# Mixer: 16 transfers for a tile of x, 8 for its latents, contiguous block transposes, and new orders of work

## The chip, the cores and the metric

One core of a Trainium2 chip runs the whole kernel in one launch. The metric is the device time of a launch in microseconds (us). All data are float32. The engines are named by what they do: TensorE multiplies matrices, VectorE and ScalarE work element by element, GpSimd helps, and the queue SP issues DMAs.

## The reference, cut to what matters

One layer of a streaming encoder over a prompt of 2048 frames and a sample of 32. The change touches its first stage only, the mixers:

```python
proj = jnp.einsum('bsd,de->bse', x, w_in)            # one projection of x for both mixers
c_q, c_kv, k_pe, pr = proj[..., :384], proj[..., 384:640], proj[..., 640:672], proj[..., 672:]
q = jnp.einsum('bsl,lhe->bshe', rms_norm(c_q, q_norm_g), w_uq)
ckv = rms_norm(c_kv, kv_norm_g)                      # the latents, also an output
kpe = apply_rope(k_pe, cos, sin)                     # also an output
attn = mla_prompt(q_nope, q_pe, ckv, kpe, w_ukv, pos)
rw, wkv_fin = rwkv7_mixer(pr, wkv0, shift0, ...)     # a recurrence, done in blocks of 64 rows
out = jnp.einsum('bsm,md->bsd', concatenate([attn, rw]), w_o)
```

Behind it come a layer norm, a top-2-of-32 mixture of experts and another layer norm.

## The kernel before

The kernel runs stage after stage: the mixer (here), attention, the router, the experts, the last norm. The mixer goes over 17 tiles of 128 rows (16 of the prompt, one with the sample). Its constants and the whole of `w_in` stay in SBUF.

Each tile passes three stages, written as Python generators: `project` (letter a) multiplies `xT`, the tile of x transposed, with `w_in`, normalises queries and latents and stores them; `rwkv` (b) does the recurrence; `heads_out` (c) normalises its heads. `layered()` joins them on every engine: a turn of the loop runs stage a of tile i, b of tile i - 1 and c of tile i - 2. Turns 0 and 1 and the two last ones (17 and 18, the drain, which have no stage a) are written out, the 15 between are a loop. Within a turn each engine's order is a string: each letter takes that stage's generator to its next `yield`. These are PE_ORDER, ACT_ORDER, VEC_ORDER and SP_ORDER, at lines 59 to 63. Engines wait for each other by named steps (`t.w(vec, "v_turned")` waits for a step of the same tile, `t.w0` for that of the tile before, `t.arrived` for a group of DMAs).

The steps that the text speaks of, by line:

- SP: first x at 519, then the weights and constants up to 536 (`w_g` at 532), the x load of later tiles in `x_load` (539 to 543), token moves of v, b and k between partitions (551), `first` and `rope` (566, 567), the stores of kpe and ckv (570, 571), of the latents to their output (`ckv_out`, 576), kpe_out (577), edge, qn and qp (581 to 591), `masks`, `keep` and `s_init` (602 to 604), and the state's store (622). In a turn SP issues the three inputs of b first, then `first` and `rope`, the tokens, kpe and ckv, the latents' stores, qn, qp, then x for the tile after next, and the state.
- VectorE: squares summed for the norms (`sq_sum`, 1067 to 1070), `pr_edge` (1075, waits for `first` and `rope`), `ckv_turned` (1097), `q_roped` (1104), `xT` (1109); the mixing of rows (1118: u_low, u_k, u_r, u_v), `u_pad` (1128, waits for masks, keep and s_init), `g_sig` (1131), `v_turned` (1136), ..., `kk_norm2` (1157), `kk_rs` (1160), `a_hat`, `b_hat`, `b_turned` (1174), `k_hat` (1177), then the levels of the block inverse (Z and U); of the heads y_centred (1245), `y_rs` (1248), `y_normed` (1250) and the gating (1253 to 1255).
- ScalarE: `cq_sq`, `ckv_sq`, kp4 (689 to 693), the copies pr3, pr1, pr0, pr2 (702), tanh, exponentials, `kk_root` (764).
- TensorE: the projection, 19 column blocks of 8 matrix products, each block in two halves (806), kpe_sum (847, waits for kp4), rms_sums (851, waits for sq_sum), q_nope and q_pe (872, 880); lora_w and lora_a (960), lora_g (967, waits for g_sig), kk_norm and bonus_sum (894), and the recurrence (901 to 1018). The group of columns k=0 needs the bank of k=3, so it waits for the copy pr3.

Every 32 columns of a VectorE transpose are turned within their 32x32 blocks. x is therefore loaded such that the blocks fall in place: rows j*4+g of the tile in partitions 32q + j.

Of the kernel before, what the change touches and what calls it, by code (L numbers as in the profile page):

```python
# [30 lines left out]
P = 128  # L31
# [8 lines left out]
CQ, CKV = QL // P, KVL // P  # L40
# [3 lines left out]
KC = D // P  # L44
# [11 lines left out]
LEVELS = 6  # L56


PE_ORDER = ("aacaabcaaaaaaabaaabaaaaaaaaaaaaaaabababbbaabaaababbbabababab"
            "abababaababbbabbbb")  # L60
ACT_ORDER = "bbbcbbcbbbaabbbbbaacaaaabbbabbb"
VEC_ORDER = "bcbbbbbcbabbbbbcabbbbbcbbbbbbbbbbbabbabababbbbbabaab"
SP_ORDER = "bbcaabbbacaaaaab"


# [318 lines left out]
def mixer(nc, io, scr):  # L384
    ahead = scr["first_of_attention"] = first_of_attention(nc)

    with ExitStack() as ctx:
        def sb(name, shape, dt=F32):
            return ctx.enter_context(nc.sbuf_tensor("mx_" + name, shape, dt))
# [24 lines left out]
        x = sb("x", [P, D])  # L414
# [7 lines left out]
        xT = sb("xT", [P, KC, P])  # L422
# [4 lines left out]
        ckv = sb("ckv", [P, CKV, P])  # L427
# [7 lines left out]
        cw, kw = sb("cw", [P, 4 * CKV, 32]), sb("kw", [32, P])  # L435
# [45 lines left out]
        first_x, first_xT = (ctx.enter_context(nc.semaphore("mx_first_" + n)) for n in ("x", "xT"))  # L481
        biases = ctx.enter_context(nc.semaphore("mx_biases"))
        selected = ctx.enter_context(nc.semaphore("mx_selected"))
        x_in = Dmas(nc, ctx, "mx_x_in", 4)
        a_in = Dmas(nc, ctx, "mx_a_in", 2)
        b_in = Dmas(nc, ctx, "mx_b_in", 3)
        mla_out = Dmas(nc, ctx, "mx_mla_out", 13, 1)
        v_in, bt_in, kt_in = (Dmas(nc, ctx, f"mx_{n}_tokens", 8, 1) for n in "vbk")
        rwkv_out = Dmas(nc, ctx, "mx_rwkv_out", 1, 1)
        edge_out = Dmas(nc, ctx, "mx_edge_out", 1, 1)  # L490
# [5 lines left out]
        def row(ap, i):  # L496
            return ap[bass.ds(i, 1)].rearrange("a p n -> p (a n)")
# [17 lines left out]
        @block.sync  # L515
        def _(sp):
            sp.dma_start(ident[:], io["ident"]).then_inc(ident_in, 16)
            for q in range(4):
                x_in.go(sp.dma_start(x[32 * q:32 * q + 32], io["x"][0, 32 * q:32 * q + 32]))
            for c0, c1 in ((0, QL + KVL), (PE_COL, PE_COL + ROPE)):  # L520
                sp.dma_start(w_in[:, :, c0:c1], w_src[:, :, c0:c1]).then_inc(w_part[4], 16)
            early.go(sp.dma_start(par[:], io["par"]))
# [15 lines left out]

            def x_load(tile):

                for q in range(4):
                    x_in.go(sp.dma_start(x[32 * q:32 * q + 32].rearrange("j (n i) -> j n i", i=32),
                                         tile.rearrange("(j g) (k a i) -> j (g k) a i", g=4, a=4, i=32)[:, :, q, :]))

            def tokens(d, dst, src):

# [10 lines left out]
            def project(t):  # L557
                t.ahead((avec, "xT", 0), (avec, "q_rope_sin", -1), (avec, "kpe_roped", 0), (avec, "ckv_turned", 0),
                        (aact, "q_nope", 0), (avec, "q_roped", 0), (aact, "edges", 0))
                i = t.i if isinstance(t.i, int) else sp.snap(t.i)  # L560
                after = i + 2 if isinstance(i, int) else sp.snap(t.i + 2)
                col = bass.ds(i * P if isinstance(i, int) else sp.snap(t.i * P), P)
                yield

                t.w0(avec, "q_rope_sin")
                a_in.go(sp.dma_start(first[:], row(io["first"], i)))
                a_in.go(sp.dma_start(rope[:], row(io["rope"], i).rearrange("p (a n) -> p a n", a=2)))
                yield
                t.w(avec, "kpe_roped")
                mla_out.go(sp.dma_start(scr["kpeT"][:, col], kpe[:]))  # L570
                mla_out.go(sp.dma_start(scr["ckvT"].rearrange("(c p) n -> p c n", p=P)[:, :, col], ckv[:]))
                t.w(avec, "ckv_turned")
                yield
                tile = io["ckv_out"][bass.ds(i, 1)].rearrange("a (i b) (c r j) -> (a i) (b c) r j", b=4, c=CKV, r=4)
                for q in range(4):
                    mla_out.go(sp.dma_start(tile[:, :, q, :], cw[32 * q:32 * q + 32]))
                mla_out.go(sp.dma_start(io["kpe_out"][bass.ds(i, 1)].rearrange("a (b i) j -> i (a b) j", b=4),
                                        kw[:].rearrange("i (b j) -> i b j", b=4)))
                yield
                t.w(aact, "edges")  # L580
                edge_out.go(sp.dma_start(row(io["edge_out"], i), edge[:].rearrange("p a n -> p (a n)")))
                yield
                t.w(aact, "q_nope")
                qd = scr["qT"]
                for h2 in range(2):
                    mla_out.go(sp.dma_start(qd.rearrange("(c b) d n -> b d c n", b=2)[h2, 0:NOPE, :, col],
                                            qn[h2 * 64:h2 * 64 + 64]))
                yield
                t.w(avec, "q_roped")
                for h4 in range(4):  # L590
                    mla_out.go(sp.dma_start(qd.rearrange("(c b) d n -> b d c n", b=4)[h4, NOPE:QK, :, col],
                                            qp[h4 * 32:h4 * 32 + 32]))
                yield
                t.w(avec, "xT")
                x_load(io["x"][bass.ds(after, 1)].rearrange("a p n -> (a p) n"))

            def rwkv(t):
# [73 lines left out]
        def _(a):  # L671
# [124 lines left out]

            layered(a, NT, (("a", 0, aact, project), ("b", 1, act, rwkv), ("c", 2, oact, heads_out)), ACT_ORDER)

        @block.tensor
        def _(pe):  # L800
# [84 lines left out]

            heads = [(q, r, slice(64 * r, 64 * r + 64)) for q in range(4) for r in range(2)]
            blocks = [(4 * c + q, q, slice(64 * c, 64 * c + 64), hs) for c in range(2) for q, _, hs in heads]

            def by_halves(dst, w, src):
# [163 lines left out]
            pe.wait_ge(w_part[4], 32)  # L1053
            layered(pe, NT, (("a", 0, aten, project), ("b", 1, ten, rwkv), ("c", 2, oten, heads_out)), PE_ORDER)

        @block.vector
        def _(v):
# [5 lines left out]
            def project(t):  # L1063
# [18 lines left out]
                for c in range(CQ):  # L1082
                    ins = v.scalar_tensor_tensor(out=cq[:, c, :], in0=b4[2][:, c, :], scalar=qg[:, c:c + 1],
                                                 in1=msr[:, 0, :], op0=ALU.mult, op1=ALU.mult)
# [3 lines left out]
                for c in range(CKV):  # L1088
                    ins = v.scalar_tensor_tensor(out=ckv[:, c, :], in0=b4[3][:, c, :], scalar=kvg[:, c:c + 1],
                                                 in1=msr[:, 1, :], op0=ALU.mult, op1=ALU.mult)  # L1090
# [3 lines left out]
                do(v.tensor_tensor(kpe[:], b4[2][32:64, 3, :], rope[32:64, 1, :], ALU.mult), "kpe_sin")  # L1094
                do(v.tensor_tensor(kpe[:], kpe[:], kpe2[0:32, :], ALU.add), "kpe_roped")
                yield
                v.transpose(cw[:].rearrange("p (b c) j -> p b c j", b=4), ckv[:].rearrange("p c (i b) -> p b c i", b=4))
                t.mark(v.transpose(kw[:], kpe[:]), "ckv_turned")
                yield

# [5 lines left out]
                t._wait(x_in, None, 1)  # L1106
                t.w(aten, "pr_proj2")
                for g in range(4):
                    ins = v.transpose(xT[:, :, g:P:4], x[:, 256 * g:256 * g + 256].rearrange("p (k i) -> p k i", k=KC))
                t.mark(ins, "xT")  # L1110

            def rwkv(t):
# [129 lines left out]
            def heads_out(t):  # L1242
# [12 lines left out]
                do(v.tensor_tensor(ys[:], ys[:], gk[:], ALU.mult), "gated")  # L1255

            layered(v, NT, (("a", 0, avec, project), ("b", 1, vec, rwkv), ("c", 2, ovec, heads_out)), VEC_ORDER)


# [1370 lines left out]
```

## Time and profile before

| | us |
|---|---|
| median of 3 runs | 3352.1 |
| lowest and highest | 3346.84, 3356.85 |
| profiled execution | 3348.55 |
| its span | 3346.5 |

The page gives, for one profiled execution, the busy time of each engine (PE is TensorE, DVE is VectorE, ACT is ScalarE, POOL is GpSimd, SPq is the queue SP that issues DMAs, PEld the weight loads) and 40 slices of the span of 83.7 us with the busy share in tenths. The mixer is slices 1 to 17 and a part of 18. The mean granted clock of TensorE over the span is 0.947.

### The profile page before, as it was taken

What the parts mean: (1) busy time and instruction counts of PE and PEld (TensorE: products, weight loads), DVE (VectorE), ACT (ScalarE), POOL (GpSimd) and SP (SyncE); (2) the same over time, 40 slices, a digit from 0 to 9 for tenths busy, and PEclk for the clock granted to TensorE, in tenths of its full rate; (3) what the DMA queues carried; (4) which work ended last, traced back from release to release, by engine and by line L of the source; (5) the groups of instructions that cost most, each with busy time, mean ns of one, the idle gap of its engine ahead of it and who ended that gap; (6) DMA issues with size and microseconds to landing.
All of it is one profiled execution on the core that took longest, in us unless ns stands there. A gap on an engine that the chain in (4) does not pass through costs nothing. (4 is left out here: it accounts for less than half of the span.)

```text
span 3346.5 us, 74487 instructions
## 1 busy us (share of the span) xinstructions
PE 2949.8 (88%) x26600; PEld 2235.1 (67%) x26601; DVE 1750.7 (52%) x3820; ACT 971.1 (29%) x2500; POOL 581.9 (17%) x875
## 2 busy tenths in 40 slices
PE   7999999999999999669898898989975999999991
PEld 6888888888888888545555555545544776666770
DVE  1666666666666666648686886822234222222225
ACT  2333333333333333224343434412210111111115
POOL 0000000000000000000000000001113555545650
PEclk9999999999999999779999999999987999999995
DMA  6111111111211111420101000033325898886447
GB/s 188 34 37 36 36 36 36 36 37 37 38 37 37 36 36 36 96 84 1 38 1 35 5 21 15 1 108 128 125 85 219 272 342 289 246 257 171 100 93 244
DMA packets 337220, 310.25 MB, mean 93 GB/s; under 512 B 235200, under 2 KB 290528, under 8 KB 322528
## 3 DMA queue, kind: packets, MB, share of 16 engines
q1 hardware_dynamic: 315424, 238.88, 23.4%
q0 software_dynamic: 21504, 67.13, 8.9%
q8 instruction: 226, 3.70, 0.5%
q14 instruction: 66, 0.54, 0.1%
HBM read 208.12 MB, written 84.42 MB: 87 GB/s over the span
## 5 line engine op out<-in xcount | busy, mean ns | idle before, releaser
L806 PE MATMUL mx_bank<-mx_xT,mx_w_in 128*128 128x128 f32 x5168 | 661.2, 286 | 71.1 <-issue 52.4
L806 PEld LDWEIGHTS mx_bank<-mx_xT,mx_w_in 128*128 128x128 f32 x5168 | 618.8, 198 | 144.1 <-issue 121.0
L1497 PE MATMUL at_bank<-pl_kT,pl_qT 128*128 128x512 f32 (+5 forms) x656 | 293.8, 534 | 2.4 <-DVE at_vals L1621 2.4
L1469 ACT ACTIVATE at_PQ<-at_bank,at_nms 128x512 f32<-128x512 f32 (+5 forms) x328 | 192.8, 596 | 277.6 <-DVE at_nms L1597 199.9
L2288 PE MATMUL ex_down<-ex_wd,ex_hT 128*128 x512 | 235.6, 603 | 28.1 <-ACT ex_hT L2217 26.4
L2165 POOL DMA_INDIRECT ex_x<-scr_hx,ex_idx x256 | 247.0, 965 | 68.3 <-issue 59.4
L2264 PE MATMUL ex_gate<-ex_wg,ex_xT 128*128 x1024 | 233.2, 381 | 19.0 <-SPq L2137 18.8
L2264 PEld LDWEIGHTS ex_gate<-ex_wg,ex_xT 128*128 128x128 f32 x1024 | 195.4, 191 | 72.9 <-issue 49.0
L2224 ACT ACTIVATE ex_y<-ex_down,ex_gcol 128x512 f32<-128x512 f32 x128 | 81.0, 683 | 543.8 <-POOL ex_gcol L2172 227.2
L2264 PE MATMUL ex_up<-ex_wu,ex_xT 128*128 x1024 | 231.6, 379 | 0.0
L1640 DVE COPY at_PT<-at_bank 128x512 f32<-128x512 f32 (+3 forms) x328 | 196.8, 601 | 55.0 <-PE at_bank L1509 41.0
L1528 PEld LDWEIGHTS at_bank<-at_PT,at_vals 128*64 128x64 f32 (+1 forms) x2208 | 118.4, 138 | 155.2 <-issue 80.9
L2333 DVE STREAM_TRANSPOSE ex_xT<-ex_x 128x256 f32<-128x256 f32 x256 | 141.1, 609 | 147.2 <-DMA ex_x<-scr_hx,ex_idx 147.2
L1509 PE MATMUL at_bank<-pl_at_ident,at_PQ 128*128 128x128 f32 x1104 | 187.4, 285 | 32.4 <-ACT at_PQ L1469 15.9
L1509 PEld LDWEIGHTS at_bank<-pl_at_ident,at_PQ 128*128 128x128 f32 x1104 | 126.8, 142 | 120.3 <-issue 57.2
L2264 PEld LDWEIGHTS ex_up<-ex_wu,ex_xT 128*128 128x128 f32 x1024 | 190.3, 191 | 23.2
L657 POOL TENSOR_TENSOR mx_AR<-mx_u,mx_ep 128x512 f32<-128x512 f32 x17 | 20.0, 1176 | 1036.2 <-DVE mx_kh L1154 1036.2
L1593 DVE TENSOR_REDUCE at_mx<-at_bank 128x1 f32<-128x512 f32 (+5 forms) x328 | 188.4, 574 | 11.8 <-PE at_bank L1497 7.3
L1528 PE MATMUL at_bank<-at_PT,at_vals 128*64 128x128 f32 (+1 forms) x2208 | 168.0, 285 | 26.0 <-DVE at_o_sb L1615 25.8
L2288 PEld LDWEIGHTS ex_down<-ex_wd,ex_hT 128*128 128x128 f32 x512 | 96.6, 192 | 132.9 <-issue 130.8
L702 ACT ACTIVATE mx_pr<-mx_bank 128x256 f32<-128x256 f32 (+1 forms) x68 | 37.0, 544 | 510.1 <-PE mx_bank L806 500.8
L2340 DVE SCALAR_TENSOR_TENSOR ex_th<-ex_th,ex_gate 128x256 f32<-128x256 f32 x64 | 26.8, 419 | 261.3 <-ACT ex_th L2212 201.0
(316 smaller groups left out, 4738.6 us busy)
## 6 DMA issues: line engine op xcount, KB each, us to landing
ex_wg<-in_w_eg SPq DMA_DIRECT2D x32, 1024.0 KB
ex_wu<-in_w_eu SPq DMA_DIRECT2D x32, 1024.0 KB
ex_wd<-in_w_ed SPq DMA_DIRECT2D x32, 1024.0 KB
mx_x<-in_x SPq DMA_DIRECT2D x76, 128.0 KB, 4.0
pl_ro_x<-in_x SPq DMA_DIRECT2D x17, 512.0 KB, 3.9
scr_hx<-ro_h SPq DMA_DIRECT2D x17, 512.0 KB, 2.7
scr_acc<-ro_ha SPq DMA_DIRECT2D x17, 512.0 KB, 2.9
co_r<-scr_acc SPq DMA_DIRECT2D x17, 512.0 KB, 5.6
```

The lines of the kernel that those rows point to most:

```text
L806: ins = pe.matmul(dst, w_in[:, k, col:col + n], xT[:, k, :], start=(k == 0), stop=(k == KC - 1))
L1469: ins = a.activation(PQ[:, n % NP, 0:full], b[:, 0:full], ACT.Exp, bias=bias, scale=SCALE, accum_out=sums[:, j, h, 1 + gi:2 + gi])
L1497: t.mark(pe.matmul(bank[n % SB][:, 0:wd], qT[h][keys(h), j * P:(j + 1) * P], kT[h][keys(h), k0 * P:k0 * P + wd], start=True, stop=True), f ...
L1509: ins = pe.transpose(bank[SB + n % TB][0:rows, c:c + P], PQ[:, n % NP, c:c + rows], ident[:, :])
L1528: ins = pe.matmul(bank[7][64 * h:64 * h + 64, 0:P], vals[0:rows, k0 + s, 64 * h:64 * h + 64], PT[0:rows, m % NPT, s, :], start=(gi == 0 an ...
L1593: t.do(v.tensor_reduce(mx[:, 1 + gi:2 + gi], b[:, 0:wd], AX.X, ALU.max), f"max{n}")
L1640: ins = v.tensor_copy(PT[:, n % NPT, 0:full, :], b[:, 0:full * P].rearrange("p (a n) -> p a n", a=full))
L2165: x_in[s].go(g.indirect_dma_start(x[s][:, k, :], None, rows, bass.IndirectOffsetOnAxis(ap=idx[s][:, k:k + 1], axis=0)))
L2224: ins = a.activation(y[s][:, 512 * n:512 * n + 512], down_b[n][:, :], ACT.Copy, scale=gcol[s][:, 0:1])
L2264: ins = pe.matmul(b[s][:, 0:FE], xT[s][:, k, :], wv[:, k * FE:(k + 1) * FE], start=(k == 0), stop=(k == KC - 1))
L2288: ins = pe.matmul(down_b[n][:, :], hT[s][:, m, :], wv[:, m * D + n * 512:m * D + (n + 1) * 512], start=(m == 0), stop=(m == FC - 1))
L2333: ins = v.transpose(xT[s][:, :, 32 * h:32 * h + 32], x[s][:, h, :].rearrange("p (i k) -> p k i", k=KC))
```

## The change

- x: each tile's load is cut by row groups as well. Where four transfers took every fourth row (partition 32q + j, row 4j + g), now sixteen take 32 consecutive rows each (row 32g + j) for one quarter q of the columns. The block transpose then writes 32 consecutive columns of `xT` instead of every fourth. The very first tile, whose rows are loaded plainly, goes from 4 transfers of 32 rows to 16 of 8 rows.
- The latents: the transpose `ckv_turned` reads and writes its tile contiguously, and the store to `ckv_out` takes 8 transfers instead of 4.
- The counts that the waits use follow: 16 DMAs for x, 17 for the stores of a tile.
- PE_ORDER, ACT_ORDER and VEC_ORDER are new strings. A new SP_ORDER is put in as well, ahead of the old line, which is still there and so is the value that holds.

```diff
-PE_ORDER = ("aacaabcaaaaaaabaaabaaaaaaaaaaaaaaabababbbaabaaababbbabababab"
-            "abababaababbbabbbb")
-ACT_ORDER = "bbbcbbcbbbaabbbbbaacaaaabbbabbb"
-VEC_ORDER = "bcbbbbbcbabbbbbcabbbbbcbbbbbbbbbbbabbabababbbbbabaab"
+PE_ORDER = ("acaaacaaaaaaabbaaaaaaaabaaaaaaaaaaaababbbababaababbbabababab"
+            "aabababababbbabbbb")
+ACT_ORDER = "bcbcbabbabbcbbabbababbaaaabbbbb"
+VEC_ORDER = "cbccbbabbbbabbbbbcbbbbbbbbbbbbbbbbabbabababbabbbbaab"
+SP_ORDER = "bbcaabbabcaaaaab"
 SP_ORDER = "bbcaabbbacaaaaab"
...
-        x_in = Dmas(nc, ctx, "mx_x_in", 4)
+        x_in = Dmas(nc, ctx, "mx_x_in", 16)
...
-        mla_out = Dmas(nc, ctx, "mx_mla_out", 13, 1)
+        mla_out = Dmas(nc, ctx, "mx_mla_out", 17, 1)
...
-            for q in range(4):
-                x_in.go(sp.dma_start(x[32 * q:32 * q + 32], io["x"][0, 32 * q:32 * q + 32]))
+            for q in range(16):
+                x_in.go(sp.dma_start(x[8 * q:8 * q + 8], io["x"][0, 8 * q:8 * q + 8]))
...
-                for q in range(4):
-                    x_in.go(sp.dma_start(x[32 * q:32 * q + 32].rearrange("j (n i) -> j n i", i=32),
-                                         tile.rearrange("(j g) (k a i) -> j (g k) a i", g=4, a=4, i=32)[:, :, q, :]))
+                for g in range(4):
+                    for q in range(4):
+                        x_in.go(sp.dma_start(x[32 * q:32 * q + 32, 256 * g:256 * g + 256].rearrange("j (k i) -> j k i", i=32),
+                                             tile[32 * g:32 * g + 32].rearrange("j (k a i) -> j k a i", a=4, i=32)[:, :, q, :]))
...
-                tile = io["ckv_out"][bass.ds(i, 1)].rearrange("a (i b) (c r j) -> (a i) (b c) r j", b=4, c=CKV, r=4)
+                tile = io["ckv_out"][bass.ds(i, 1)].rearrange("a (b i) (c r j) -> i (a b) c r j", b=4, c=CKV, r=4)
                 for q in range(4):
-                    mla_out.go(sp.dma_start(tile[:, :, q, :], cw[32 * q:32 * q + 32]))
+                    for c in range(CKV):
+                        mla_out.go(sp.dma_start(tile[:, :, c, q, :], cw[32 * q:32 * q + 32, 4 * c:4 * c + 4, :]))
...
-                v.transpose(cw[:].rearrange("p (b c) j -> p b c j", b=4), ckv[:].rearrange("p c (i b) -> p b c i", b=4))
+                v.transpose(cw[:].rearrange("p n j -> p (n j)"), ckv[:].rearrange("p c n -> p (c n)"))
...
-                    ins = v.transpose(xT[:, :, g:P:4], x[:, 256 * g:256 * g + 256].rearrange("p (k i) -> p k i", k=KC))
+                    ins = v.transpose(xT[:, :, 32 * g:32 * g + 32], x[:, 256 * g:256 * g + 256].rearrange("p (k i) -> p k i", k=KC))
```

## Rows read from the trace of the kernel before

**Rows 1.** The page, part 2: TensorE's busy tenths in 40 slices.

```profile
PE   7999999999999999669898898989975999999991
```

**Rows 2.** Waits of TensorE, 150 to 1300 us: us in total, times, longest.

```profile
PE mx_bank L806 <- issue: 52.4, 14, 3.9
...
PE mx_bank L847 <- ACT mx_kp L693: 6.4, 14, 1.5
PE mx_bank L851 <- DVE mx_sq L1070: 4.9, 7, 1.2
```

**Rows 3.** Timeline of TensorE, one turn: start us, us, instructions, [idle before <-releaser].

```profile
716.87 3.59 PE L806 MATMUL mx_bank<-mx_xT,mx_w_in 128*128 128x128 f32 x16 [3.63 <-issue]
...
731.71 1.06 PE L967 MATMUL mx_bank<-mx_sg,mx_w_g 128*128 128x128 f32 x8
...
734.18 0.49 PE L851 MATMUL mx_bank<-mx_sq,mx_rmsw 128*128 128x128 f32 x2 [0.53 <-DVE mx_sq L1070]
```

**Rows 4.** Timelines of TensorE: starts of the 2nd, 3rd, 9th and 15th turn of the loop.

```profile
225.86 3.78 PE L806 MATMUL mx_bank<-mx_xT,mx_w_in 128*128 128x128 f32 x16 [3.67 <-issue]
...
307.81 3.78 PE L806 MATMUL mx_bank<-mx_xT,mx_w_in 128*128 128x128 f32 x16 [3.78 <-issue]
...
798.31 3.49 PE L806 MATMUL mx_bank<-mx_xT,mx_w_in 128*128 128x128 f32 x16 [3.82 <-issue]
...
1288.88 2.41 PE L806 MATMUL mx_bank<-mx_xT,mx_w_in 128*128 128x128 f32 x15 [3.75 <-issue]
```

**Rows 5.** Windows: us, busy (instructions) of PE, PEld, DVE, ACT, POOL, clock, DMA, GB/s.

```profile
229.00:232.00 3.00, 3.00 (x9) 1.17 (x9) 0.42 (x1) 0.00 (x0) 0.00 (x0) 0.50 0.48 114
...
720.00:723.00 3.00, 3.00 (x22) 2.07 (x21) 1.36 (x4) 0.76 (x2) 0.00 (x0) 0.98 0.37 96
```

**Rows 6.** Timeline of VectorE in the same turn.

```profile
710.94 2.04 DVE L1109 STREAM_TRANSPOSE mx_xT<-mx_x 128x256 f32<-128x256 f32 x4 [0.22 <-DVE mx_qp L1104]
...
725.46 0.17 DVE L1128 TENSOR_TENSOR mx_u<-mx_u,mx_masks 128x4 f32<-128x4 f32 x1 [2.00 <-DMA mx_s_init<-in_s_init]
...
729.24 3.35 DVE L1248 RECIPROCAL mx_yq<-mx_yq 128x512 f32<-128x512 f32 x1
...
732.71 0.71 DVE L1136 STREAM_TRANSPOSE mx_SA<-mx_u 128x512 f32<-128x512 f32 x1
```

**Rows 7.** Timeline of the queue SP in the same turn.

```profile
707.81 0.46 SPq L577 DMA_DIRECT2D out_kpe_out<-mx_kw  x1
...
714.00 3.99 SPq L542 DMA_DIRECT2D mx_x<-in_x  x4
718.09 1.99 SPq L622 DMA_DIRECT2D out_state_out<-mx_S  x1
...
722.10 0.38 SPq L604 DMA_DIRECT2D mx_s_init<-in_s_init  x1
...
754.80 5.19 SPq L551 DMA_DIRECT2D mx_kt<-mx_t  x8
```

**Rows 8.** Timelines of the start: SP, ScalarE, TensorE and VectorE.

```profile
1.17 1.80 SPq L519 DMA_DIRECT2D mx_x<-in_x  x4
...
28.28 14.40 SPq L542 DMA_DIRECT2D mx_x<-in_x  x4
...
21.63 0.21 ACT L677 ACTIVATE mx_negh<-mx_par 128x8 f32<-128x8 f32 x1 [13.61 <-DMA mx_w_g<-in_w_g]
...
36.33 25.22 PE L806 MATMUL mx_bank<-mx_xT,mx_w_in 128*128 128x128 f32 x224
...
46.21 0.24 DVE L1075 SCALAR_TENSOR_TENSOR mx_pr<-mx_pr,mx_first 128x14 f32<-128x14 f32 x1 [10.69 <-DMA mx_rope<-in_rope]
```

**Rows 9.** Timelines of tile 1: u_pad on VectorE, lora_g on TensorE.

```profile
77.36 0.17 DVE L1128 TENSOR_TENSOR mx_u<-mx_u,mx_masks 128x4 f32<-128x4 f32 x1 [5.25 <-DMA mx_s_init<-in_s_init]
...
83.08 1.06 PE L967 MATMUL mx_bank<-mx_sg,mx_w_g 128*128 128x128 f32 x8
```

**Rows 10.** Timeline of VectorE in the drain: u_pad and kk_rs.

```profile
1374.66 0.17 DVE L1128 TENSOR_TENSOR mx_u<-mx_u,mx_masks 128x4 f32<-128x4 f32 x1 [3.53 <-DMA mx_s_init<-in_s_init]
...
1388.51 3.35 DVE L1160 RECIPROCAL mx_t<-mx_t 128x512 f32<-128x512 f32 x1 [1.08 <-ACT mx_t L764]
```

## The prediction

> **What bounds the kernel now.** I read the page first: its 40 slices say that the Mixer, the stretch that the change touches, fills the first 17 slices and that TensorE is 90% or more busy in nearly all of them [rows 1]. So VectorE's time, which the change cuts, matters only where TensorE waits for it. Next the view of waits, for TensorE inside the tile loop: in 14 turns it lost 52.4 us to "issue" (the return to the loop's top, about 3.7 us each turn, with no releaser), 6.4 us to ScalarE's copy kp4 and 4.9 us to VectorE's sum of squares [rows 2]. That is all that an order could win there besides short waits on SA that keep their place: 11.3 us over 14 turns, 0.8 us a turn. Then the timelines of one turn, tile by tile: TensorE starts the turn at 716.87, comes to lora_g at 731.71 and has its last stall before the sum of squares at 734.18 [rows 3]. The turns start 81.77 us apart on average: (1288.88 - 225.86) / 13 [rows 4].
>
> One more thing costs time in each turn. After the gap at the loop's top the granted clock is 0.50 (1.2 GHz). In the turn that began at 225.86 it is still 0.50 between 229 and 232; in the one that began at 716.87 it is 0.98 from 720 on [rows 5]. A turn thus starts with some 6 or some 3 us at half speed and loses about 3 or 1.5 us. The turn from 225.86 to 307.81, with the long stretch, took 81.95 us, the one from 716.87 to 798.31 took 81.44 us [rows 3, 4], with more stalls in it.
>
> **The transposes.** Four of them make xT in 2.04 us, strided by four elements; a contiguous one of twice the width (v_turned) took 0.71 us [rows 6]. Half the width contiguous is about 0.40 us with its fixed part, so four take about 1.4 us (bounds: 2.0, if the stride is free, and 1.2) and the one on the latents saves 0.2 us. VectorE gains some 0.9 us a tile. In the loop xT is finished at 712.98 and TensorE starts only at 716.87 after y1 ended at about 713.2, so this is worth nothing there: the loop's return covers it. Without that cover it would be worth at most 0.6 us. It counts once, between tiles 0 and 1, where TensorE does wait for xT: -0.6 us.
>
> The Trainium skill (SBUF — State Buffer, in the section on the DMA port swizzle) says that a stride of up to four fp32 elements is free. By it the transposes would not shorten and the sum would be 0.6 us more. The trace speaks against it, since 256 strided elements cost 0.51 us (2.04 / 4) beside 0.71 us for 512 contiguous ones, but it could be another fixed part; nothing in the sum below hangs on it.
>
> **The queue SP.** This is where the change costs. Its order does not change: the diff adds a new SP_ORDER, but the old line stands behind it and holds. x_load goes from 4 issues to 16, the latents' store from 4 to 8, with the same bytes and, for x, the same 128-byte runs. What does one issue cost? The token moves have 32 partitions by 8 runs, exactly the shape of a new x load: 5.19 us for 8, 0.65 us each, with fixed addresses. The four x loads now have four times the runs and took 3.99 us, one of them blocked for 1.5 us and three at 0.82 us with their address arithmetic. The kpe store (32 by 4 runs, the shape of a new latent store) took 0.46 us [rows 7]. So the price goes by the issue and not by the runs: I take 0.82 us for an x load in the loop (bounds 0.65 and 1.0), 0.65 to 0.74 outside it, 0.65 us for a latent store.
>
> In the loop x_load then takes 16 x 0.82 = 13.1 us for 4.0. Behind it in SP's queue stand the state's store, masks, keep and s_init, then first and rope. VectorE waits for s_init before u_pad: it was released at 725.46, for an issue at 722.10 [rows 6, 7]. The new issue: 9.1 us later for x, about 0.9 us earlier since the loads' first no longer queues behind blocked ones, and 1.6 us earlier because the state's store (1.99 us, blocked by the x traffic) goes back to about 0.4 (the issue of s_init, as many bytes, took 0.38): 728.7. With a landing of 3.3 us as now, or down to 1 us less without the blocked traffic ahead, u_pad comes at 731.0 to 732.0, 6 us later. The latent stores' extra 1.5 us costs nothing: ckv_turned moves ahead of U4, Z5 and U5 in VectorE's order, and SP has to wait for q_roped anyway.
>
> Who waits for that? The new VEC_ORDER puts y_rs (3.35 us) and y_normed ahead of u_k, so VectorE fills most of the delay. g_sig follows u_pad by 0.45 us: 731.5 to 732.5. TensorE comes to lora_g with the same work ahead of it as before, at 731.71 (lora_w moved down next to it, all ten projection halves ahead of it stay). Stall: 0 to 0.8 us. In return lora_g now no longer finishes before kp4 and the squares are there: ScalarE takes cq_sq and ckv_sq before the tanh work, so kp4 is ready at about 731.4 and the sum of squares at 732.3 to 733.3, for TensorE at 732.8 and 733.2. The two old stalls, 0.8 us a turn, go. Later links that I followed: kk_norm is asked for 3.7 us later and is ready; kk_rs starts some 4 us later, bonus_sum is two halves later and has about 0.7 us to spare behind GpSimd's rkr; gram_k, U_start and Z1 keep 0.4 us or more. So a turn's work shrinks by 0.8 us, less the stall at lora_g.
>
> Not all of it comes out. A turn that starts earlier against the clock's changes meets the long or the short slow stretch differently, and the turn with the long one lasted longer though it stalled less. I take -0.6 us a turn, bounds -1.0 (the whole stall and a little clock) and +0.5 (the stall at lora_g outweighs them). Over 15 turns: -9 us, from -15 to +8.
>
> **The start.** The first x goes from 4 issues (1.80 us) to 16, 12 x 0.45 = 5.4 us more, ahead of every weight. ScalarE waited until 21.63 for the last constant, w_g, and TensorE's first projection behind it [rows 8]. The loads between are bound by bandwidth and x lies out of their way earlier, so I take +4.6 us (3.8 to 5.4). Then x for tile 1: its four issues took 14.40 us because the queue was full of weights, and rope, behind them, released pr_edge at 46.21; TensorE runs 25.22 us of projections from 36.33 and needs pr3, which needs pr_edge, after 12 halves, at about 47.1 [rows 8]. Here there is only about 0.5 us of slack. 12 more issues at 0.65 us are 7.8 us if all come after the block, about 3 if most are taken in by then; I take +4.5 us of stall (2.5 to 7.5).
>
> Tile 1: s_init released u_pad at 77.36, TensorE came to lora_g at 83.08 [rows 9]. With 12 x 0.74 = 8.9 us more, u_pad comes at 86.2 and g_sig at 86.7, 3.4 us after lora_g could begin. Both move together with what lies ahead. Sum of the start: 4.6 + 4.5 + 3.4 - 0.6 = +11.9 us, from 6 to 16.
>
> **The drain.** After the last turn no projection covers the chain. u_pad waited until 1374.66; the 12 extra issues (12 x 0.8 us, less what was blocked) make it about 1382.7, +8.0. But y_rs and y_normed (3.35 us and some 1 us), which stood between u_v and kk_rs, are now done while it waits, and the gating moves ahead of kk_rs (+1.4) from behind b_turned (-1.4). ScalarE's Sqrt for kk_root needs its table again behind both exponentials, and it released kk_rs at 1388.51 [rows 10]; by the queues in order I get 1393.0 for kk_rs, +4.5, and 1.4 us back behind b_turned: +3.1 us (0 to 6).
>
> **The sum.** 11.9 - 9 + 3.1 = +6 us. The profiled execution took 3348.55 us, so 3354.6 on its own scale. It lies 3.5 us under the median of the three runs, 3352.1, and I set the forecast on the median: 3358.
>
> **Rivals.** (1) The x issues become the bound of the loop. g_sig meets lora_g when an issue costs 0.82 us; each 0.06 us more moves it by 1 us, and TensorE stalls by that in every turn, now uncovered. For it: the old mean is 1.0 us an issue, and the queue was blocked by x traffic. Against it: three of four cost 0.82, and the traffic is now spread over 13 us. At 0.90 us: 1.3 us x 15 = 20 us on top, 3378; at 1.0 us 3400 or more. (2) The start costs only its lower end (+6), the drain nothing, and the clock gives back what the stalls did, -1.2 us a turn: 6 - 18 = -12 us, 3340. For it: of the two turns above, the one with the short slow stretch is 0.5 us shorter in spite of its stalls. Against it: a turn can fall back to the long stretch, as the earlier turn shows. (3) The change does for VectorE what it says and the rest cancels: 3350 to 3353. VectorE is not the bound, and only the issues' places count.
>
> Against the change also speaks the Trainium skill (DMA: Bandwidth & Descriptors, rules for kernel authors): many small transfers should be joined, under 64 KB one pays mostly overhead. That is rival 1 in general; the token rows bear out the fixed price of an issue, 0.65 us for 32 KB.
>
> **Chances.** Forecast (3345 to 3366) 0.53; rival 1 0.22; rival 2 0.13; rival 3 0.12. What a measurement of this kernel can tell from no change is about 0.3%, 10 us. Faster by more than that: rival 2 mostly, 0.12. Slower by more: rival 1 and the upper part of the forecast, 0.37. Within: 0.51. The range 3339 to 3384 holds the forecast with its bounds, most of rival 2 and rival 1 up to 0.92 us an issue.
>
> **What would show it.** Start: ScalarE's first copy after w_g at about 26 instead of 21.6, TensorE's third projection group late behind pr_edge, lora_g of tile 1 late. Loop: x loads in about 13 us a turn, u_pad released by s_init some 14 to 15 us after the turn's start instead of 8.6, the stalls on kp4 and on the squares gone, lora_g's stall at 0 to 0.8. Drain: kk_rs about 3 to 5 us later against the last turn. The prediction is wrong if an x issue costs over 0.88 us, if a link that I left with under 1 us (rkr, Z1) stalls, or if the turns' length follows the clock another way.

## The result

| | before | after |
|---|---|---|
| median | 3349.55 us (4 runs) | 3376.01 us (4 runs, 3375.53 to 3386.53) |
| profiled execution | 3348.55 us | 3375.53 us |
| its span | 3346.5 us | 3373.5 us |
| ratio of the times | | 1.0083, 95% interval 1.0057 to 1.0109 |

The changed kernel is slower by 0.8%, some 27 us. The forecast was 3358 us, 6 us slower and most probably too little to measure. The time is inside the stated range (3339 to 3384) but above the band of 3345 to 3366 that had a chance of 0.53; slower by more than 10 us had 0.37.

The page after, parts 1 and 2 (busy us, share of the span, instructions; then TensorE in 40 slices):

```profile
PE 2963.5 (88%) x26600; PEld 2243.5 (67%) x26601; DVE 1736.7 (51%) x3820; ACT 979.7 (29%) x2500; POOL 581.9 (17%) x875
...
PE   6999999999999999668888898989975999999991
```

VectorE has become faster, 1736.7 us for 1750.7, as the change says. That the kernel is slower all the same agrees with [rows 1]: TensorE still fills the Mixer's slices, and VectorE's time is not what ends last.

**Where the 27 us lie.** Four marks in the trace divide the span. The second turn of the loop starts at 238.89 (before 225.86 [rows 4]): +13.0. The last turn starts at 1311.26, so 13 turns take 1072.37 us for 1063.02: +9.4. From there to the end of the last gating it is 171.0 us for 166.3: +4.6. What follows the Mixer takes 1891.3 us in both. Together +27.0.

The waits of TensorE between 150 and 1300 us (us in total, times, longest), beside [rows 2]:

```profile
PE mx_bank L809 <- issue: 45.1, 13, 3.7
PE mx_bank L970 <- DVE mx_sg L1134: 16.2, 10, 3.0
PE mx_bank L940 <- ACT mx_SA L779: 8.1, 14, 0.6
```

The stalls on kp4 (6.4 us) and on the squares (4.9 us) are gone, as forecast. A new one stands in their place: lora_g waits for VectorE's g_sig (mx_sg) in 10 turns, 16.2 us in all.

Two turns of the 13, timeline of TensorE (start us, us, instructions, [idle before <- releaser]):

```profile
653.10 1.15 PE L809 MATMUL mx_bank<-mx_xT,mx_w_in 128*128 128x128 f32 x8 [3.38 <-issue]
...
669.31 2.08 PE L970 MATMUL mx_bank<-mx_sg,mx_w_g 128*128 128x128 f32 x8 [2.76 <-DVE mx_sg L1134]
...
737.41 2.07 PE L809 MATMUL mx_bank<-mx_xT,mx_w_in 128*128 128x128 f32 x8 [3.50 <-issue]
...
753.85 1.16 PE L970 MATMUL mx_bank<-mx_sg,mx_w_g 128*128 128x128 f32 x8
```

The first turn starts at full speed: eight matmuls take 1.15 us. TensorE is at lora_g 13.4 us after its start, finds nothing, and waits 2.76 us. Behind the wait eight matmuls of the same size take 2.08 us: the clock has gone to its lower level, as the window behind the stall shows too. The turn lasts 84.3 us. The next turn starts at half speed (2.07 us), begins lora_g only 16.4 us after its start, with next to no wait (0.09 us), and lasts 81.73 us.

The other turns are of both kinds. Four of the 13 wait 1.75 to 2.76 us at lora_g, have a second stretch at half speed behind the wait, and last 83.2 to 84.3 us. The nine others wait 1.2 us or less, have no second stretch, and last 81.1 to 82.7 us. Both turns that start at full speed (at 403.75 and 653.10) are among the four.

```profile
669.00:672.00 3.00, 2.69 (x11) 2.14 (x11) 2.75 (x9) 3.00 (x9) 0.00 (x0) 0.50 0.21 50
```

The seventh figure of this row of the windows, 0.50, is the granted clock, 1.2 GHz for 2.4.

VectorE and the queue SP in the same stretch, to be read beside [rows 6, 7]:

```profile
668.74 0.17 DVE L1131 TENSOR_TENSOR mx_u<-mx_u,mx_masks 128x4 f32<-128x4 f32 x1 [3.49 <-DMA mx_s_init<-in_s_init]
...
731.59 1.42 DVE L1112 STREAM_TRANSPOSE mx_xT<-mx_x 128x256 f32<-128x256 f32 x4 [0.22 <-DVE mx_qp L1107]
...
747.11 3.35 DVE L1251 RECIPROCAL mx_yq<-mx_yq 128x512 f32<-128x512 f32 x1 [3.90 <-ACT mx_yq L793]
...
753.28 0.17 DVE L1131 TENSOR_TENSOR mx_u<-mx_u,mx_masks 128x4 f32<-128x4 f32 x1 [0.82 <-DMA mx_s_init<-in_s_init]
```

```profile
650.16 13.80 SPq L544 DMA_DIRECT2D mx_x<-in_x  x16
...
666.64 0.38 SPq L607 DMA_DIRECT2D mx_s_init<-in_s_init  x1
...
718.61 4.43 SPq L579 DMA_DIRECT2D out_ckv_out<-mx_cw  x8
...
731.53 3.04 SPq L594 DMA_DIRECT2D scr_qT<-mx_qp  x4
734.77 13.70 SPq L544 DMA_DIRECT2D mx_x<-in_x  x16
748.56 0.55 SPq L625 DMA_DIRECT2D out_state_out<-mx_S  x1
751.14 0.38 SPq L607 DMA_DIRECT2D mx_s_init<-in_s_init  x1
```

The 16 x loads keep the queue for 13.70 us, 0.86 us each. s_init is issued only then, u_pad (line 1131) waits for it until 15.6 us and 15.9 us into the two turns (8.6 before; 14.7 to 17.1 over the 13 turns), and g_sig and lora_g stand behind u_pad.

### The profile page after: what moved, and what is told of

Read it like the earlier page. It is cut to its first block and busy times, and to the rows that moved or that the text cites. A ratio compares the mean times of both kernels' runs of the same rounds, so it can differ in the third digit from the quotient of the medians.

```text
span 3373.5 us, 75263 instructions
## 1 busy us (share of the span) xinstructions
PE 2963.5 (88%) x26600; PEld 2243.5 (67%) x26601; DVE 1736.7 (51%) x3820; ACT 979.7 (29%) x2500; POOL 581.9 (17%) x875
## 5 line engine op out<-in xcount | busy, mean ns | idle before, releaser
L1447 POOL TENSOR_TENSOR at_PQ<-at_zero 64x64 f32<-64x64 f32 x128 | 36.1, 284 | 681.1 <-PE at_bank L1512 680.8
```

## The experiments

The kernels of one block ran on the same chip and share its runs of the kernel before; ratios are to these. A turn's length is the time from the second to the fifteenth start of a turn, divided by 13, and the clock is the mean granted clock of that stretch. The kernel before has 81.77 us and 0.97, the changed one 82.49 us and 0.96 in its first profile. Turn and clock are those of one profiled execution: kernels with nearly the same median differ in them by up to 1 us (79.52 for best, 80.47 for transposes_only), so a difference of 2 us is read as a finding and one of 0.5 us is not.

| kernel | median | ratio, 95% interval | turn | clock |
|---|---|---|---|---|
| old_orders | 3533.58 | 1.0521, 1.0497 to 1.0546 | 91.95 | 0.91 |
| new_orders_only | 3328.08 | 0.9908, 0.9888 to 0.9928 | 79.65 | 0.99 |
| b_in_first | 3339.29 | 0.9942, 0.9921 to 0.9964 | 79.82 | 0.98 |
| rope_first | 3377.46 | 1.0053, 1.0035 to 1.0072 | 82.52 | 0.96 |
| transposes_only | 3326.95 | 0.9903, 0.9887 to 0.9920 | 80.47 | 0.98 |
| head_swapped | 3331.48 | 0.9921, 0.9905 to 0.9938 | 80.20 | 0.98 |
| after_again (the changed kernel) | 3386.37 | 1.0091, 1.0067 to 1.0116 | 82.92 | 0.96 |
| all_three | 3331.01 | 0.9919, 0.9902 to 0.9935 | 80.61 | 0.97 |
| twelve_tiny | 3408.86 | 1.0152, 1.0135 to 1.0169 | 84.06 | 0.95 |
| best | 3325.33 | 0.9906, 0.9889 to 0.9922 | 79.52 | 0.99 |
| old_orders_b_in_first | 3351.79 | 0.9986, 0.9976 to 0.9995 | 81.71 | 0.96 |

The kernel before took 3359.34 us in the first block (the first four), 3356.77 in the second (the next four) and 3357.89 in the third.

**First block: split the change, and test the cause.** old_orders is the changed kernel with the instruction orders of before; new_orders_only is the kernel before with the new orders.

```diff
-PE_ORDER, ACT_ORDER, VEC_ORDER   (the new strings)
+PE_ORDER, ACT_ORDER, VEC_ORDER   (those of the kernel before)
```

> The changed transfers and transposes with the old PE_ORDER, ACT_ORDER and VEC_ORDER. Theory 1 (the 12 extra x issues delay s_init and with it u_pad and g_sig): now y_rs no longer fills VectorE's wait, so besides lora_g also bonus_sum comes to wait, some 2 us a turn: about 3395 to 3410 us, slower than the change. Theory 2 (the new orders themselves cost the time, the transfers little but the start): 3360 to 3368 us, faster than the change.

It took 3533.58 us, far above what was expected. Its waits of TensorE, and VectorE in one turn:

```profile
PE mx_bank L853 <- DVE mx_sq L1072: 73.4, 13, 6.6
PE mx_bank L808 <- issue: 41.6, 12, 3.7
PE mx_bank L969 <- DVE mx_sg L1133: 34.5, 13, 3.1
```

```profile
821.28 0.17 DVE L1130 TENSOR_TENSOR mx_u<-mx_u,mx_masks 128x4 f32<-128x4 f32 x1 [10.78 <-DMA mx_s_init<-in_s_init]
...
825.05 3.35 DVE L1250 RECIPROCAL mx_yq<-mx_yq 128x512 f32<-128x512 f32 x1
...
829.66 0.28 DVE L1072 TENSOR_TENSOR mx_sq<-mx_sq 128x128 f32<-128x128 f32 x1
```

In the old order y_rs (line 1250) and the sum of squares stand behind u_pad. VectorE idles 10.78 us for s_init, and then everything that it could have done meanwhile comes late: TensorE waits some 5.6 us for the squares in each turn. The expectation counted lora_g and bonus_sum, some 2 us a turn, and left out the squares.

This run also shows that the two parts of the change do not add up. With the old orders the transfers cost 5.2% (1.0521), with the new ones 1.8% (1.0083 over the 0.9908 of the next run): the new VectorE order does work during the wait for s_init that in the old one stands behind it.

> The kernel before with the three new orders and nothing else (4 transfers for x, strided transposes). Theory 1: no stall at lora_g, and those on kp4 and on the squares gone as well, start unchanged: 3338 to 3347 us, a little faster than before. Theory 2: slower than before, 3358 us or more.

```diff
-PE_ORDER, ACT_ORDER, VEC_ORDER   (those of the kernel before)
+PE_ORDER, ACT_ORDER, VEC_ORDER   (the new strings)
```

```profile
PE mx_bank L807 <- issue: 48.6, 18, 3.7
PE mx_bank L938 <- ACT mx_SA L777: 8.1, 14, 0.6
```

3328.08 us, 31 us under the kernel before on this chip. Expected were 5 to 14 us under the 3352.1 us that it had on the first chip. The new orders are the gain and the transfers the loss. No wait but the loop's top and SA is left, and the turn is 2.12 us shorter, though the stalls that went were 0.8 us a turn [rows 2]. The windows of this kernel's 13 turns (after the stretch: its us, PE, PEld, DVE, ACT, POOL busy, clock, DMA share, GB/s) show another part of it, a mean clock of 0.99 for 0.97. The first row is the start of its first turn here, at full speed; the kernel before has no such turn among its 13:

```profile
221.83:224.83 3.00, 3.00 (x20) 2.07 (x21) 0.69 (x1) 0.07 (x1) 0.00 (x0) 1.00 0.77 124
...
221.83:1257.32 1035.49, 982.37 (x14119) 877.40 (x14119) 657.81 (x1183) 342.77 (x780) 68.27 (x52) 0.99 0.19 38
```

The same row of the kernel before and of the changed one:

```profile
225.86:1288.88 1063.02, 998.06 (x14118) 891.94 (x14119) 656.64 (x1183) 335.12 (x781) 68.26 (x52) 0.97 0.19 37
```

```profile
238.89:1311.26 1072.37, 1006.10 (x14118) 895.34 (x14119) 645.88 (x1183) 342.79 (x780) 68.28 (x52) 0.96 0.19 36
```

TensorE's work is the same in the three (14118 or 14119 matmuls), but it is busy for 982, 998 and 1006 us. These 24 us between the best and the worst are clock, not work. Per turn, the 2.12 us that the new orders gain are 1.21 us less busy and 0.91 us less idle time; the 2.84 us that the transfers then cost are 1.83 us more busy and 1.01 us more idle time.

**b_in_first**: the changed kernel, with masks, keep and s_init issued ahead of the x loads instead of behind them.

```diff
+                if not (isinstance(t.i, int) and t.i == 0):
+                    t.w0(vec, "state_in")
+                b_load(i)                     # masks, keep, s_init
                 ...
                 x_load(...)
                 ...
-                t.w0(vec, "state_in")
-                b_in.go(...)                  # masks, keep, s_init
```

> The change, but masks, keep and s_init of the next turn are issued ahead of the x loads instead of behind them. Theory 1: u_pad no longer waits for s_init, the stalls at lora_g go in the loop, in turns 1 and 2 and in the drain: 3350 to 3360 us, some 20 us under the change. Theory 2: within 5 us of the change, 3371 to 3381 us.

It took 3339.29 us: 0.9942 of the kernel before, where the changed kernel had 1.0083 and 1.0091. In its queue SP and on VectorE:

```profile
631.30 0.38 SPq L560 DMA_DIRECT2D mx_s_init<-in_s_init  x1
631.88 12.97 SPq L544 DMA_DIRECT2D mx_x<-in_x  x16
```

```profile
644.90 0.17 DVE L1136 TENSOR_TENSOR mx_u<-mx_u,mx_masks 128x4 f32<-128x4 f32 x1
```

```profile
PE mx_bank L814 <- issue: 46.8, 14, 3.6
PE mx_bank L945 <- ACT mx_SA L784: 8.6, 15, 0.6
PE mx_bank L902 <- POOL mx_t L669: 0.6, 1, 0.6
```

u_pad waits for nothing, lora_g's stall is gone, and the turn falls from 82.49 to 79.82 us, with all 16 x loads still in it. That is the theory's main proof: it is not the 16 transfers but what stands behind them in the queue. It gives back 1.4 to 1.5% of the time, 47 to 50 us, more than twice the 20 us that were expected.

**rope_first**: the changed kernel, with tile 1's x loads issued behind first and rope of tile 0.

```diff
-            x_load(io["x"][1])                # ahead of the loop
                 ...
+                if isinstance(t.i, int) and t.i == 0:
+                    x_load(io["x"][1])        # behind rope's issue
```

> The change, but tile 1's x is issued behind first and rope of tile 0 instead of ahead of them. Theory 1: TensorE's stall of 4.8 us behind pr3 in the first tile goes, the loop is as in the change: 3370 to 3373 us. Were the start's cost the late weights alone, it would stay at 3376.

The stall of 4.78 us behind pr3 is gone. Tile 0 takes 46.53 us from its first projection to that of tile 1, for 54.05; tile 1 starts at 73.31 for 78.72, though the first projection was 2.1 us later in this execution, and the loop's second turn starts at 234.85 for 238.89. The whole took 3377.46 us, ratio 1.0053 for 1.0083. The turns are as long as before the edit:

```profile
PE mx_bank L971 <- DVE mx_sg L1135: 22.2, 12, 3.4
```

The start's loss is real and separate, some 4 us at the mark for this part. Its interval (1.0035 to 1.0072) overlaps that of the changed kernel, so the total alone would not show it; the times of the marks do.

**Second block.** transposes_only is new_orders_only with the two contiguous block transposes, and with 4 and 4 transfers. It leaves out the regrouping of rows that the extra transfers do, so its tokens stand in another order than the reference's.

```diff
-v.transpose(xT[:, :, g:P:4], x[...])
+v.transpose(xT[:, :, 32 * g:32 * g + 32], x[...])
```

> The kernel before with the new orders and with the contiguous transposes, but still with 4 transfers for x and 4 for the latents. It leaves out the regrouping of rows that the transfers would have to do, so the rows of a tile stand in another order and the outputs are not the reference's; the work of every engine is the same. Theory 1 (VectorE's transposes are hidden, only the first tile's xT is waited for): within 2 us of the kernel with the new orders alone, which took 3328 us beside 3359 us for the kernel before: ratio to before 0.989 to 0.992. Rival (the shorter transposes are worth their 0.9 us in each of 17 tiles): 0.986 or less.

3326.95 us, 0.9903, beside 0.9908 without them in the first block: what the extra transfers are there for is worth nothing that can be measured here. The transposes themselves are faster (1.42 us for 2.04 us for the four of x, 0.43 us for 0.63 us for the latents' one), but those of x lie under the gap at the loop's top and nothing is seen to wait for the latents' one.

**head_swapped** asks why the new orders shorten a turn by 2.1 us. It gives new_orders_only a start of the turn as in the old string.

```diff
-PE_ORDER = ("acaaac...
+PE_ORDER = ("aacaac...
```

> The kernel before with the new orders, but TensorE's turn begins with two projection halves and then y_mean, as in the old order, instead of half, y_mean, half. Theory A (the clock's loss at the loop's top depends on how the first work after the gap is broken up): the turns go from 79.7 to over 81 us, ratio to before 0.995 to 1.0. Theory B (the new orders gain because the stalls on kp4 and on the squares are gone): the turns stay at 79.4 to 80.0 us, ratio 0.989 to 0.993.

0.9921 and 80.20 us a turn: the intervals of the two overlap. The first letters of TensorE's order are not what makes most of the 2.1 us.

**after_again** is the changed kernel once more, to have it on this chip.

> The changed kernel itself, to compare on the same chip. 0.6 to 1.0% slower than before; turns of 82.5 us on average, stalls at lora_g in most of them.

3386.37 us, 1.0091: it repeats. The turn took 82.92 us here.

**all_three**: b_in_first and rope_first together, and tile 0's x in 4 transfers; in the loop x still has 16.

```diff
-            for q in range(16):
-                x_in.go(sp.dma_start(x[8 * q:8 * q + 8], ...))
+            for q in range(4):
+                sp.dma_start(x[32 * q:32 * q + 32], ...).then_inc(x_in.sem, 64)
```

> The change with masks, keep and s_init ahead of the x loads, tile 1's x behind rope, and the very first x in 4 transfers. Theory 1: b_in_first's gain (ratio to before 0.994) and the stall behind pr3 (4.8 us) and the later weights (2 us) gone as well: ratio 0.991 to 0.993. If start and loop were not additive, as b_in_first, 0.994.

3331.01 us, 0.9919. The first projection is at 21.13 for 24.68 and nothing stalls behind pr3. So the changed kernel, with all its transfers in the loop, can run within 4 us of transposes_only, which ran on the same chip. Of the 55 us between this kernel and after_again nearly all is a matter of where the issues stand; the 12 issues fewer for tile 0 are the rest.

**Third block.** **twelve_tiny** separates the number of issues from the bytes and from the transposes: new_orders_only, with 12 loads of 2 KB each (32 partitions by 8 runs of 8 bytes) behind its 4 x loads.

```diff
+                for c in range(12):
+                    x_in.go(sp.dma_start(tiny[:, c], tile[0:32].rearrange("j (k i) -> j k i", k=8)[:, :, 2 * c:2 * c + 2]))
```

> The kernel before with the new orders, 4 transfers for x, and behind them twelve further loads of 32 partitions by 8 runs of 8 bytes from the same tile into a buffer that nobody reads. Theory 1 (what costs is the number of issues between xT and s_init, not the bytes nor how x is cut): s_init as late as in the change, lora_g stalls, turns of 82 to 83 us from 80, about 40 us (ratio to before 1.000 to 1.008; the start is partly dearer too). Rival (the cutting of x itself, its traffic, costs): turns stay near 80 us, ratio 0.990 to 0.994.

```profile
745.51 3.83 SPq L544 DMA_DIRECT2D mx_x<-in_x  x4
749.43 10.51 SPq L547 DMA_DIRECT2D mx_tiny<-in_x  x12
...
762.62 0.38 SPq L608 DMA_DIRECT2D mx_s_init<-in_s_init  x1
```

```profile
PE mx_bank L810 <- issue: 44.0, 13, 3.7
PE mx_bank L971 <- DVE mx_sg L1135: 28.8, 14, 4.0
```

3408.86 us, 1.0152, against 0.9908 without the tiny loads. 12 loads that move almost nothing cost 0.88 us each in the queue and 82 us in all (0.0244 x 3358), twice the 40 us that were expected. It is more than the change lost: the loads hold the queue for 14.4 us instead of 13.7, lora_g stalls for 28.8 us instead of 16.2, and the loop's second turn starts at 244.39 for 221.83, since the tiny loads stand ahead of rope at the start too. The issue is the price, and not the bytes. A load of x in the same fence has four times as many runs as a tiny one and takes hardly longer (3.83 / 4 = 0.96 us, beside 0.88).

**best**: new_orders_only with the two moves, s_init ahead of x and tile 1's x behind rope, 4 transfers.

> The kernel before with the new orders, masks, keep and s_init ahead of the x loads, and tile 1's x behind rope. In new_orders_only u_pad does not wait for s_init in the loop, so nothing is left to gain there but in the drain (u_pad some us earlier): 0 to 5 us under new_orders_only, ratio to before 0.988 to 0.992. If it is the fastest of all it beats both kernels.

3325.33 us, 0.9906: faster than both kernels, and the same as new_orders_only. Once the queue is short, its order no longer makes a difference that is seen here.

**old_orders_b_in_first**: the kernel before, with masks, keep and s_init ahead of x.

> The kernel before with its old orders, masks, keep and s_init ahead of the x loads. Theory B (the new orders gain what TensorE loses on kp4 and on the squares, and the clock follows): u_pad's wait of 2 us goes, the stall on the squares (4.9 us over 14 turns) with it, that on kp4 stays: 5 to 12 us under before, ratio 0.996 to 0.999. If the orders gain in another way, no change beyond 3 us: 0.999 to 1.001.

```profile
PE mx_bank L811 <- issue: 51.9, 14, 3.9
PE mx_bank L852 <- ACT mx_kp L698: 7.1, 14, 1.5
```

```profile
224.80:1287.06 1062.26, 1001.03 (x14118) 892.61 (x14119) 657.08 (x1183) 335.31 (x781) 68.30 (x52) 0.96 0.19 37
```

3351.79 us, 0.9986 (10 runs). The squares' stall (4.9 us [rows 2]) is gone, and by the ratio the kernel is 4.7 us faster (1.7 to 8.1): the stall came out about whole. The turn of the profiled execution, 81.71 for 81.77 us, doesn't show it. There the mean clock is 0.96 for 0.97 and TensorE is busy 3 us longer, and two executions of one kernel differ by as much (1006.1 us in the changed kernel, 1009.5 in after_again). So the early s_init is not what makes the new orders quick: it gives about 5 us and they give 31.

## Why the prediction was right and wrong

**The start: right.** Forecast +11.9 us up to tile 1, and tile 2 starts 11.25 us later (155.78 for 144.53); the mark of +13.0 us holds the loop's first turn too. The terms were partly off and made up for one another. Timelines of TensorE and of the queue SP after, beside [rows 8, 9]:

```profile
24.68 8.26 PE L809 MATMUL mx_bank<-mx_xT,mx_w_in 128*128 128x128 f32 x48 [14.32 <-DVEq L287]
54.49 15.98 PE L809 MATMUL mx_bank<-mx_xT,mx_w_in 128*128 128x128 f32 x128 [4.78 <-ACT mx_pr L705]
78.72 8.53 PE L809 MATMUL mx_bank<-mx_xT,mx_w_in 128*128 128x128 f32 x48 [2.90 <-DVE mx_xT L1112]
94.22 1.16 PE L970 MATMUL mx_bank<-mx_sg,mx_w_g 128*128 128x128 f32 x8 [1.54 <-DVE mx_sg L1134]
```

```profile
1.16 5.45 SPq L520 DMA_DIRECT2D mx_x<-in_x  x16
...
32.75 17.81 SPq L544 DMA_DIRECT2D mx_x<-in_x  x16
```

The first projection came 2.1 us later (24.68 for 22.62), not 4.6. That is partly chance of the two executions: over all traces it is at 24.7 to 27.0 us in the five kernels with 16 issues and at 21.0 to 23.8 us in the eight with 4, 4.2 us apart in the mean, near the forecast. The 16 issues took 5.45 us for 1.80, 3.65 us more, where the sum had 5.4. pr3 stalled by 4.78 us, forecast 4.5. The matmuls behind that stall ran partly at half speed (granted clock 0.50 from 54.5 to 57.5) and took 1.6 us more, which I had not counted. The wait for xT fell from 3.45 to 2.90 us (forecast -0.6, measured -0.55). lora_g of tile 1 waited 1.54 us for a forecast of 3.4, as the tile also began with some 6 us at half speed (before: some 3); the one of the next tile, the loop's first turn, waited 2.98 us.

**The transposes: right.** 1.42 us for four where the estimate was 1.4, and nothing of it counts in the loop (transposes_only). The Trainium skill (SBUF — State Buffer, in the section on the DMA port swizzle) says that a stride of up to four fp32 elements is free. The measurement decides against it here: the same 256 elements, strided by four, cost 0.51 us (2.04 / 4) and contiguous 0.36 us (1.42 / 4), the latter in transposes_only too, where only the transposes differ.

**The loop: wrong, and it is the term that failed.** Forecast -0.6 us a turn, -9 us in all over 15 turns; measured +0.72 us a turn, 82.49 for 81.77, which is +9.4 us over the 13 turns between the marks, and +1.8 us for the loop's first turn. The prediction made this of two parts, and both were mis-sized, in opposite directions:

| part, us a turn | forecast | measured |
|---|---|---|
| the new orders | -0.8 (the stalls that go) | -2.12 (new_orders_only, 79.65) |
| the transfers, over the new orders | 0 to +0.8 at lora_g, +0.2 taken | +2.84 (82.49 - 79.65) |

With the spread of a turn among like kernels (79.5 to 80.6 us with the new orders and no stall) the first is between -1.2 and -2.2 and the second between +1.9 and +3.0; neither comes near its forecast. That the two errors have opposite signs is luck, and it is why the total still fell inside the range.

*The delay of s_init.* The chain was the right one (x loads, s_init, u_pad, g_sig, lora_g), and its stall was to be 0 to 0.8 us. It was 1.0 us a turn on average over the 13 turns and up to 2.8 (16.2 us over the 14 turns of the view, with the 2.98 us of the first). Three small errors, all to the same side: an x load took 0.86 us and not 0.82, 0.6 us over 16; the x loads began 2.6 to 2.9 us ahead of the turn's start where I had 3.8, as qp's four issues ahead of them take 3.0 us, about 1 us; and TensorE needs lora_g 13.4 us after a quick start, not the 14.84 us of [rows 3], a turn with a slow stretch, 1.4 us. u_pad itself came 14.7 to 17.1 us into the turn, forecast 14 to 15. This is rival 1 in mechanism, at a price between its 0.82 and its 0.90 us an issue. Even its time is the one measured, 3378 us at 0.90 us an issue for 3376, but by luck: the stall differs from turn to turn (0 to 2.8 us), and its sum (6 + 20 us) got there without the gain of the orders.

*The clock.* 1.0 us of stalls does not make 2.84 us. The rest, 1.8 us a turn, is busy time at half speed: TensorE is busy 24 us longer over the 13 turns for the same matmuls. Since one execution is a small sample, here are the means of the three traces with the late s_init and the new orders (the changed kernel, after_again, rope_first) beside the six with the new orders and no stall (new_orders_only, b_in_first, transposes_only, head_swapped, all_three, best). The turn is 82.6 us beside 80.0, 2.6 us longer; the stall at lora_g is 1.3 us, and TensorE is busy 1.4 us longer. By the granted clock along the turns, about half of this 1.4 us (0.7 us) comes from the second stretch at half speed behind the stall, which none of the six kernels has, and the rest (0.6 us) from longer stretches at half speed behind the loop's top. Why those are longer is not shown.

The prediction said that the clock takes something of what the stalls give. It had not asked what a new stall does to the clock, or what an order without any stall would win there. b_in_first shows both at once: the stall at lora_g goes, 1.0 us, and the turn falls by 2.67 us.

The forecast had the orders' gain at the removed stalls alone, 0.8 us; the prediction's rival 2 had -1.2 us a turn and the clock as its reason, and some of it was still missing.

**The drain: right in kind.** Forecast +3.1 us, measured +4.6. VectorE there:

```profile
1406.64 0.17 DVE L1131 TENSOR_TENSOR mx_u<-mx_u,mx_masks 128x4 f32<-128x4 f32 x1 [6.46 <-DMA mx_s_init<-in_s_init]
...
1417.10 3.35 DVE L1163 RECIPROCAL mx_t<-mx_t 128x512 f32<-128x512 f32 x1 [0.35 <-ACT mx_t L767]
```

kk_rs is at 1417.10 for 1388.51 [rows 10], and the last turn started 22.38 us later: 6.2 us late against that start, where the forecast had 4.5. 1.6 us (6.2 - 4.6) come back until the last gating ends (forecast 1.4).

**The stores.** 8 latent stores took 4.43 us for 3.59 with 4 and cost TensorE nothing, as forecast.

**What the loss consists of.** From the experiments' ratios and 3358 us: the new orders -31 us (0.9908). The issues ahead of s_init +47 to +50 us (b_in_first against the changed kernel). The start, with tile 1's x ahead of rope and tile 0's in 16, some +8 us (0.9942 to 0.9919, all_three). What is left between all_three and transposes_only is 4 us, which the measurement can't tell from nothing. The sum is +28 to +31 us, or 24 to 27 without the last; 27 us were measured on the first chip and 30 (after_again) on the second.

**What stays open.** Why the new orders shorten a turn by 2.12 us (1.2 to 2.2 by the like kernels) when the stalls that they remove are 0.8 us. More than half of it, 1.21 us, is TensorE's busy time, and the traces show where: behind the loop's top. Of the 13 turns of the kernel before, eight start with 5 to 6 us at half speed and five with some 3. Of those of new_orders_only, five start at full speed and eight with some 3 us. The gap at the loop's top is also shorter (3.26 us for 3.74 us, the mean over the turns). That the gap's length decides how long the clock stays down is not shown: after_again has gaps of 3.44 us in the mean and mostly long stretches, transposes_only 3.48 us and mostly short ones. Neither the head of TensorE's order (head_swapped) nor the early s_init (old_orders_b_in_first) brings the gain about. Which letters of the three strings do was not tried.

## What to carry to other kernels

Before a transfer is cut in pieces, count the issues that stand behind it in its queue, and look for who waits for the last of them: here 12 more issues at 0.86 us put off a load that has nothing to do with them, and moving that load ahead gave back 47 to 50 us at no cost that is seen. Price a stall by what it does to the clock too: on this kernel 1.3 us of stall a turn went with turns 2.6 us longer. And split a change that has two parts before judging it: this one hid a gain of 0.9% behind a loss of 1.8%. The parts need not add up: without the new orders the same transfers cost 5.2%.

## What the runs showed of the hardware

- The time to issue a transfer on the queue SP went by the issue and hardly by the bytes: 0.86 us for an x load of 32 KB with computed addresses (13.70 / 16), 0.88 us for a load of 2 KB in as many runs (10.51 / 12), 0.34 us for one of whole rows at the start (5.45 / 16). Whether the computed addresses make the difference was not tried.
- The granted clock fell to 0.50 (1.2 GHz) behind a stall of 2.76 us at lora_g, though TensorE had run at full speed in the 13.4 us since the turn's start. In the three traces with the late s_init and the new orders, all 14 turns with a stall of 1.68 to 3.66 us there have such a second slow stretch, and none of the 25 with 1.46 us or less. A turn that began at half speed came to lora_g nearly without a stall and was the shorter one, 81.73 for 84.3 us.
- Small stalls removed gave back unlike amounts. In the old orders the 4.9 us of the squares came out as 4.7 us (1.7 to 8.1) of the whole time (old_orders_b_in_first). With the new orders 11.3 us of stalls went and 31 us came out, at a mean clock of 0.99 for 0.97 (new_orders_only).
